# Four moves in VectorE's program order in the attention part of a decoder step

## The chip, the cores and the metric

The kernel runs on one core of a Trainium2 chip. The metric is the device time of one execution in microseconds (us). Engines in the rows: PE is TensorE (matmuls and transposes), PEld its weight loads, DVE VectorE, ACT ScalarE, POOL GpSimd, SP SyncE, whose queue issues the DMAs. Each engine runs its own program in the written order and meets the others at semaphores.

## The reference

One decoder layer for 1024 prompt tokens and for 8 sample tokens, each of which looks back at 1024 cached positions in 8 pages of 128. What matters here is the attention of the prompt, and the scores of the cached pages:

```python
z = h @ w_in                                   # q, k, v of 4 differential and 8 forgetting heads
q1, q2, ka = rope(q1), rope(q2), rope(k)       # rotation, differential heads alone
a  = softmax(q1 k1^T) - lam * softmax(q2 k2^T);  oa = a @ v        # differential group
s  = q k^T + C[t] - C[s];                        of = softmax(s) @ v   # forgetting group
# each sample token: the same against its 8 cached pages, C from the cached log gates
x  = x + rmsnorm(concat(rmsnorm(oa), of) @ w_o)
x  = x + rmsnorm((gelu(conv(h @ w_gate)) * (h @ w_up)) @ w_down)
```

Everything is float32; the large products are made as three products of a high and a low part.

## The kernel before, in words

All four engines walk through the same 64 jobs, `for J in range(NJ + 3)`. Job J is the block of 128 queries `tile(J) = J % 8` against the keys up to it, in unit `unit(J) = J // 8`. A unit is a pair of head maps. Units 0 to 3 are the differential heads, units 4 to 7 the forgetting heads (`fox(J)`, J from 32 on). A job's work is spread over several rounds:

- TensorE in round J: the scores of job J (line 1361), half chunks of the input projection of a later unit (line 1271), transposes of keys and values into rows (1385), the weighted sum of job J-2 (1413, or 1410 in the forgetting units), small matmuls for the sample tokens (1423 to 1443), value pages (1455), and at the round's end the transposes of job J-1's weights (`turn`, 1397). In the forgetting units the result of job J-3 is turned back (1495), and the second map of job J-2 is transposed near the round's start.
- VectorE in round J: the row maxima of job J (1120), the reciprocals and scales of job J-1 (`weights`, 1087 to 1096), the scaled result rows of job J-2 (`rows_out`, 1109 or 1106), in the forgetting units the copies of the second map's transposed weights (`turned`, 1127, into `a_t`), and the reduction of one key page (1044).
- ScalarE: exponentials (859), copies of the first map's transposed weights (853), the copies of the projection's chunks out of PSUM (745 to 755), their half swap (764) and rows (836, 847).
- GpSimd: the product of each key page with the queries (`multiply`, 641, four pieces to a page), the sums of log gates over later pages (`later_pages`, 652), low parts of weights (614), and from unit 1 on the rotations.

Two things tie the order of these together. First, nearly all small results of TensorE go through two PSUM banks in turn, in the order of a list `ring`. TensorE takes the bank of entry n only when entry n-2 has been copied out (`bank(e)`, `wait_evacuated`). In a round the end of the list is: the weighted sum `("o", J-2)`, the small sample entries, the page sums `("fb", b)`, then one or two entries for the transposes of job J-1, one for each four blocks. So the second of two such entries lies in the bank of `("fb", b)`, if there is one in that round. Page sums fall in rounds 4, 11, 18, 25, 32, 39, 46 and 54. Second, key pages lie in two buffers: a page is loaded when the page before the last has been reduced, multiplied by GpSimd, then reduced by VectorE in a fixed round.

The keys of unit 1 are projected in rounds 0 to 2, and VectorE rotates them (`rope`, lines 974 to 978, three instructions to a third). `behind_first` names rounds 39, 47 and 55, whose page work is done in the round that follows, behind the first maximum.

Of the kernel before, what the change touches and what calls it, by code (L numbers as in the profile page):

```python
# [29 lines left out]
PAGES = 8  # L30
PAST = PAGES * P
NPOOL = DB * PAGES * 5 // 4
MAPS = 8
# [129 lines left out]
def project(nc, io, place):  # L163
# [117 lines left out]
    NJ = MAPS * NT  # L281
# [96 lines left out]
    def bank_of(e):  # L378
        return PS[:, 4 + X[e] % 2, :]
# [57 lines left out]
    with nc.Block() as block:  # L437
# [503 lines left out]
        def _(dve):  # L941
# [181 lines left out]
            def turned(J):  # L1123
                for e in turns_of(J, 1):
                    _, _, m, c, nblk = e
                    dve.wait_ge(x_done, X[e] + 1)
                    dve.tensor_copy(at[:, m, c:c + nblk, :], bank_of(e)[:, 0:nblk * P].rearrange("p (k q) -> p k q", q=P)).then_inc(dve_evac, 1)
# [21 lines left out]
            def pages_and_norms(J):  # L1149
                for g in range(2, EARLY_PAGES) if J == 0 else k_pages(J - 1):  # L1150
                    if not late_page(g):
                        reduce_page(g)
                for b in at_job(J, 1):
                    page_maxima(b)

            behind_first = [4 * NT + NT - 1, 5 * NT + NT - 1, 6 * NT + NT - 1]
            for J in range(NJ + 3):
                if J >= 3 and fox(J - 3):
                    rows_out(J - 3)
                if J < LAST_UNIT:  # L1160
                    maximum(J, 0)
                if J - 1 in behind_first and J < LAST_UNIT:
                    pages_and_norms(J - 1)
                if 2 <= J < NJ + 2 and fox(J - 2):
                    turned(J - 2)
                if LAST_UNIT <= J < NJ:
                    maximum(J, 0)
                if J - 1 in behind_first and J == LAST_UNIT:
                    pages_and_norms(J - 1)
                if J < NJ:  # L1170
                    maximum(J, 1)
                if 1 <= J <= NJ:
                    weights(J - 1)
                if 2 <= J < NJ + 2 and not fox(J - 2):
# [21 lines left out]
                if J == 1:  # L1196
# [1 line left out]
                    dve.wait_ge(w_hi_done, n + 1)  # L1198
                    dve.wait_ge(w_lo_done, n)
                    dve.tensor_tensor(w_lo[:, n % 2], w_raw[:, n % 2], w_hi[:, n % 2].bitcast(F32), ALU.subtract).then_inc(w_lo_done, 1)  # L1200
                if 1 <= J <= 3:
                    rope(chunk_of(k_tile(1), J - 1))
                if J < NJ:
                    for e in soft_at(J):
                        if e[0] == "fb":
                            dve.wait_ge(x_done, X[e] + 1)
                            if e[1]:
                                dve.wait_ge(fb_added, e[1])
                            dve.tensor_copy(gate_sum.rearrange("p n m -> p (n m)"), bank_of(e)[:, 0:PAGES * MAPS]).then_inc(dve_evac, 1)
                        elif e[0] == "mt":  # L1210
                            row_maximum(e[1])
                        elif e[0] == "nm":
# [1692 lines left out]
```

## Time and profile before

| | before |
|---|---|
| median of 3 runs | 1432.31 us (1429.55 to 1434.42) |
| the profiled execution, its own time | 1437.39 us |
| its span, first to last instruction | 1434.4 us |
| mean granted clock of TensorE | 0.996 of full |
| granted clock of TensorE from 480 to 500 us | 1.00 of full |
| TensorE matmuls, busy | 1393.1 us, 97% |
| VectorE, busy | 896.3 us, 62% |

The span is one execution; the runs are timed without the profiler. 3.0 us of the profiled execution lie outside its span. The attention rounds go from about 148 us to about 620 us of the span. An instruction's row gives its start, its duration, and in brackets how long its engine had been idle before it and what ended that. Starts on one engine may lie up to some tenths of a microsecond ahead of the end of the instruction before, since the ends are partly drain.

### The profile page before, as it was taken

The page shows a single profiled execution, that of the slowest core. Times are in us where ns is not written, and L with a number is a line of the kernel's source. Part 1 is how long each engine was busy: PE and PEld are TensorE (multiplying, and loading weights), DVE is VectorE, ACT ScalarE, POOL GpSimd, SP SyncE. Part 2 cuts the span into 40 slices and gives each one's busy share as a digit, 9 for nine tenths or more (in the row PEclk, how much of TensorE's full clock was granted, in tenths as well). Part 3 has the DMA queues.
Part 4 walks back from the last instruction along what each step waited for, and adds up shares of the span by engine and source line. Part 5 has one row for each costly group of instructions (what it writes and reads, how often), then busy time and mean ns, then how long its engine had stood idle before and what let it go on. Part 6 is the DMA issues. An engine that isn't in the chain of part 4 may idle for free. (4 is left out here: it accounts for less than half of the span.)

```text
span 1434.4 us, 27861 instructions
## 1 busy us (share of the span) xinstructions
PE 1393.1 (97%) x10628; PEld 1256.8 (88%) x10628; DVE 896.3 (62%) x1437; ACT 630.6 (44%) x1216; POOL 521.0 (36%) x727
## 2 busy tenths in 40 slices
PE   7999999999999999899999999999999998999998
PEld 6999877877777777577899899999999998999998
DVE  6421767667565654675459767766776657654685
ACT  7743655554454454633334423332333223444552
POOL 4223777765555650011103143344332425100052
PEclk9999999999999999999999999999999999999999
DMA  6113557777767663531322254555454527656773
GB/s 193 45 50 90 177 165 223 220 233 253 249 199 223 200 218 93 199 133 61 103 83 89 82 155 141 154 155 157 137 151 141 155 97 251 176 164 197 231 257 109
DMA packets 219390, 229.78 MB, mean 160 GB/s; under 512 B 24739, under 2 KB 151531, under 8 KB 219220
## 3 DMA queue, kind: packets, MB, share of 16 engines
q1 hardware_dynamic: 219258, 228.01, 51.5%
q8 instruction: 84, 1.38, 0.4%
q14 instruction: 48, 0.39, 0.1%
HBM read 181.06 MB, written 46.99 MB: 159 GB/s over the span
## 5 line engine op out<-in xcount | busy, mean ns | idle before, releaser
L641 POOL TENSOR_TENSOR k_page<-k_page,q_bc 128x256 f32<-128x256 f32 x256 | 184.9, 754 | 136.7 <-DMA k_page<-in_cache_fox_k 101.3
L1271 PE MATMUL PS<-ht_hi,w_hi 128*128 128x344 f32 x576 | 193.9, 337 | 2.3 <-DVE ht_lo L950 1.4
L1271 PE MATMUL PS<-ht_hi,w_lo 128*128 128x344 f32 x576 | 184.6, 320 | 0.0
L1271 PE MATMUL PS<-ht_lo,w_hi 128*128 128x344 f32 x576 | 184.3, 320 | 0.0
L2772 PE MATMUL PS<-act_hi,wd_hi 128*128 128x258 f32 x616 | 140.8, 287 | 7.7 <-DVE act_lo L2575 7.1
L859 ACT ACTIVATE probs<-probs,stat 128x256 f32<-128x256 f32 (+7 forms) x128 | 98.5, 771 | 98.7 <-DVE stat L1120 98.0
L2772 PE MATMUL PS<-act_hi,wd_lo 128*128 128x258 f32 x616 | 139.0, 284 | 0.0
L2772 PE MATMUL PS<-act_lo,wd_hi 128*128 128x258 f32 x616 | 138.8, 284 | 0.0
L1271 PEld LDWEIGHTS PS<-ht_hi,w_hi 128*128 128x128 f32 x576 | 109.0, 189 | 27.3 <-issue 20.3
L2720 PE MATMUL PS<-ht_hi,wgu_hi 128*128 128x258 f32 x608 | 122.7, 283 | 0.0
L2720 PE MATMUL PS<-ht_lo,wgu_hi 128*128 128x258 f32 x608 | 122.5, 283 | 0.0
L2720 PE MATMUL PS<-ht_hi,wgu_lo 128*128 128x258 f32 x608 | 122.5, 283 | 0.0
L2349 ACT ACTIVATE conv<-gate,conv_consts 128x1032 f32<-128x1032 f32 x22 | 27.5, 1252 | 206.3 <-DVE gate L2537 186.3
L2772 PEld LDWEIGHTS PS<-act_hi,wd_hi 128*128 128x128 f32 x616 | 102.1, 191 | 9.2 <-DVE act_lo L2575 9.2
L1271 PEld LDWEIGHTS PS<-ht_lo,w_hi 128*128 128x128 f32 x576 | 108.9, 189 | 0.0
L1271 PEld LDWEIGHTS PS<-ht_hi,w_lo 128*128 128x128 f32 x576 | 108.6, 189 | 0.0
L2772 PEld LDWEIGHTS PS<-act_lo,wd_hi 128*128 128x128 f32 x616 | 102.2, 190 | 0.0
L2772 PEld LDWEIGHTS PS<-act_hi,wd_lo 128*128 128x128 f32 x616 | 102.0, 191 | 0.0
L1044 DVE TENSOR_REDUCE scores<-k_page 128x16 f32<-128x1024 f32 x64 | 77.3, 1210 | 33.0 <-POOL k_page L641 33.0
L2720 PE MATMUL PS<-t_hi,wgu_hi 128*128 128x258 f32 x456 | 93.1, 286 | 3.5 <-DVE u L2537 3.5
L2720 PEld LDWEIGHTS PS<-ht_hi,wgu_lo 128*128 128x128 f32 x608 | 94.3, 189 | 0.0
L2720 PEld LDWEIGHTS PS<-ht_hi,wgu_hi 128*128 128x128 f32 x608 | 94.3, 190 | 0.0
(311 smaller groups left out, 3357.8 us busy)
## 6 DMA issues: line engine op xcount, KB each, us to landing
b_dram<-conv SPq DMA_DIRECT2D x77, 258.0 KB, 3.1
k_page<-in_cache_diff_k SPq DMA_DIRECT2D x64, 256.0 KB, 2.9
k_page<-in_cache_fox_k SPq DMA_DIRECT2D x64, 256.0 KB, 3.4
v_page<-in_cache_diff_v SPq DMA_DIRECT2D x64, 256.0 KB, 2.8
v_page<-in_cache_fox_v SPq DMA_DIRECT2D x64, 256.0 KB, 3.0
act_raw<-b_dram SPq DMA_DIRECT2D x55, 258.0 KB, 2.7
w_raw<-in_w_in SPq DMA_DIRECT2D x24, 512.0 KB, 5.3
wgu_raw<-in_w_gate SPq DMA_DIRECT2D x22, 512.0 KB, 4.5
```

Source lines behind the costliest of these rows:

```text
L641: ins = pool.tensor_tensor(kpage[:, g % 2, c:c + PIECE], kpage[:, g % 2, c:c + PIECE], qbc[:, c:c + PIECE], ALU.mult)
L859: act.activation(p, p, ACT.Exp, bias=stat[:, J % 8, m:m + 1], scale=-1.0, accum_out=stat[:, J % 8, 2 + m:3 + m]).then_inc(exp_done, 1)
L1044: dve.tensor_reduce(scores[:, b % 3, :, n, :], kpage[:, g % 2, :].rearrange("p (k m c) -> p k m c", k=2, c=HD), AX, ALU.add).then_inc(red_ ...
L1271: ins = pe.matmul(PS[:, z_bank(c), 0:THIRD], b[:, k, :], a[:, k, third(i)], start=(k == 0 and p == 0), stop=(k == KC - 1 and p == 2))
L2349: act.activation(cbuf[:, f % 2, :], gb[:, f % 2, 2:2 + TOK], ACT.Identity, bias=bias[:, f:f + 1], scale=taps[2][:, f:f + 1]).then_inc(c_in ...
L2720: ins = pe.matmul(PS[:, bank + piece, 0:PART], w[:, k, :], a[:, k, piece * PART:(piece + 1) * PART], start=first and k == 0 and m == 0, st ...
L2772: ins = pe.matmul(PS[:, bank_of(r, d) + piece, 0:PART], w[:, d * P:(d + 1) * P], a[:, first + piece * PART:first + (piece + 1) * PART], st ...
```

## The change

Only VectorE's program is written in another order; no instruction is added or taken away.

1. The three rotations of unit 1's keys move from the ends of rounds 1, 2 and 3 to rounds 2, 3 and 4, behind both maxima and ahead of the reciprocals.
2. In all rounds with page sums but 39, the copy of the page sums (`gate_sums`) moves behind the page reductions of that round.
3. In rounds 40 and 48 the copies into `a_t` (`turned(J - 2)`) move ahead of the page reduction and of what follows it.

```diff
@@ def pages_and_norms(J)
                 for b in at_job(J, 1):
+                    if J not in behind_first:
+                        gate_sums(("fb", b))
                     page_maxima(b)
+
+            def gate_sums(e):
+                dve.wait_ge(x_done, X[e] + 1)
+                if e[1]:
+                    dve.wait_ge(fb_added, e[1])
+                dve.tensor_copy(gate_sum..., bank_of(e)[:, 0:PAGES * MAPS]).then_inc(dve_evac, 1)
@@ for J in range(NJ + 3)
                 if J < LAST_UNIT:
                     maximum(J, 0)
+                if 2 <= J < NJ + 2 and fox(J - 2):
+                    turned(J - 2)
                 if J - 1 in behind_first and J < LAST_UNIT:
                     pages_and_norms(J - 1)
-                if 2 <= J < NJ + 2 and fox(J - 2):
-                    turned(J - 2)
...
                 if J < NJ:
                     maximum(J, 1)
+                if 2 <= J <= 4:
+                    rope(chunk_of(k_tile(1), J - 2))
                 if 1 <= J <= NJ:
                     weights(J - 1)
...
-                if 1 <= J <= 3:
-                    rope(chunk_of(k_tile(1), J - 1))
                 if J < NJ:
                     for e in soft_at(J):
                         if e[0] == "fb":
-                            dve.wait_ge(x_done, X[e] + 1)
-                            ...
+                            if J in behind_first:
+                                gate_sums(e)
```

VectorE, end of round 3 and start of round 4, before: the rotation (974 to 978), the page reduction (1044), the maxima of job 4 (1120), then the weights of job 3.

```order
L1109 TENSOR_SCALAR q_t_64<-PS,stat_106 128x128
L974 TENSOR_TENSOR z_raw_104<-z_raw_104,cos_81 128x344
L975 TENSOR_TENSOR z_swapped_105<-z_swapped_105,sin_82 128x344
L978 TENSOR_TENSOR k_t_70<-z_raw_104,z_swapped_105 128x344
L1044 TENSOR_REDUCE scores_99<-k_page_95 128x2x8
L1120 ISA probs_77,stat_106<-PS,zeros_mask_86 128x640
L1120 ISA stat_106 128x1
L1120 ISA probs_77,stat_106<-PS,zeros_mask_86 128x640
L1120 ISA stat_106 128x1
L1087 RECIPROCAL stat_106<-stat_106 128x2
```

The same place in the changed kernel:

```order
L1109 TENSOR_SCALAR q_t_64<-PS,stat_106 128x128
L1044 TENSOR_REDUCE scores_99<-k_page_95 128x2x8
L1120 ISA probs_77,stat_106<-PS,zeros_mask_86 128x640
L1120 ISA stat_106 128x1
L1120 ISA probs_77,stat_106<-PS,zeros_mask_86 128x640
L1120 ISA stat_106 128x1
L974 TENSOR_TENSOR z_raw_104<-z_raw_104,cos_81 128x344
L975 TENSOR_TENSOR z_swapped_105<-z_swapped_105,sin_82 128x344
L978 TENSOR_TENSOR k_t_70<-z_raw_104,z_swapped_105 128x344
L1087 RECIPROCAL stat_106<-stat_106 128x2
```

The rotation stands now between the maxima and the weights; rounds 2 and 3 read the same with other widths.

VectorE, end of round 32, before: the scaled rows (1109), the copy of the page sums, the reduction of the last page of sample token 4, its maxima, and job 33.

```order
L1109 TENSOR_SCALAR q_t_64<-PS,stat_106 128x128
L1209 COPY sample_gate_sums_59<-PS 128x64
L1044 TENSOR_REDUCE scores_99<-k_page_95 128x2x8
L1050 TENSOR_TENSOR scores_99<-scores_99,sample_gate_sums_59 128x64
L1054 TENSOR_REDUCE page_max_122<-scores_99 128x16
L1120 ISA probs_77,stat_106<-PS,gate_34_83 128x256
```

The same place in the changed kernel:

```order
L1109 TENSOR_SCALAR q_t_64<-PS,stat_106 128x128
L1044 TENSOR_REDUCE scores_99<-k_page_95 128x2x8
L1162 COPY sample_gate_sums_59<-PS 128x64
L1050 TENSOR_TENSOR scores_99<-scores_99,sample_gate_sums_59 128x64
L1054 TENSOR_REDUCE page_max_122<-scores_99 128x16
L1120 ISA probs_77,stat_106<-PS,gate_34_83 128x256
```

The copy, which gives TensorE its bank back, stands behind the reduction. In rounds 4, 11, 18, 25 and 54 it is the same; in round 46 two reductions stand ahead of it.

VectorE, start of round 48, before: the first maximum, the reduction, the two copies into `a_t`, the second maximum.

```order
L1120 ISA probs_77,stat_106<-PS,gate_34_83 128x128
L1120 ISA stat_106 128x1
L1044 TENSOR_REDUCE scores_99<-k_page_95 128x2x8
L1127 COPY a_t_80<-PS 128x512
L1127 COPY a_t_80<-PS 128x384
L1120 ISA probs_77,stat_106<-PS,gate_35_84 128x128
```

The same place in the changed kernel:

```order
L1120 ISA probs_77,stat_106<-PS,gate_34_83 128x128
L1120 ISA stat_106 128x1
L1127 COPY a_t_80<-PS 128x512
L1127 COPY a_t_80<-PS 128x384
L1044 TENSOR_REDUCE scores_99<-k_page_95 128x2x8
L1120 ISA probs_77,stat_106<-PS,gate_35_84 128x128
```

The copies stand ahead of the reduction. In round 40 the page sums' addition and maxima stand there too, and they move with the reduction.

## Rows read from the trace of the kernel before

**Rows 1.** The page's first part: busy time, share of the span, instructions.

```profile
PE 1393.1 (97%) x10628; PEld 1256.8 (88%) x10628; DVE 896.3 (62%) x1437; ACT 630.6 (44%) x1216; POOL 521.0 (36%) x727
```

**Rows 2.** TensorE's waits, 145 to 600 us: releaser, total, times, longest.

```profile
PE PS L1397 <- DVE q_t L1109: 1.7, 2, 1.1
```

**Rows 3.** Timeline of VectorE, rounds 1 to 4: start, duration, instruction, idle time.

```profile
158.77 1.03 DVE L974 TENSOR_TENSOR z_raw<-z_raw,cos 128x344 f32<-128x344 f32 x1
161.66 1.21 DVE L1044 TENSOR_REDUCE scores<-k_page 128x16 f32<-128x1024 f32 x1
...
163.74 0.15 DVE L1087 RECIPROCAL stat<-stat 128x2 f32<-128x2 f32 x1
164.24 0.48 DVE L1096 SCALAR_TENSOR_TENSOR probs<-probs,stat 128x256 f32<-128x256 f32 x1
164.90 0.51 DVE L974 TENSOR_TENSOR z_raw<-z_raw,cos 128x344 f32<-128x344 f32 x1
...
171.59 1.21 DVE L1044 TENSOR_REDUCE scores<-k_page 128x16 f32<-128x1024 f32 x1
173.16 0.83 DVE L1120 CUSTOM_DVE_ANT_0 probs<-PS,zeros_mask 128x640 f32<-128x640 f32 x1 [0.35 <-PE PS L1361]
174.65 0.16 DVE L1087 RECIPROCAL stat<-stat 128x2 f32<-128x2 f32 x1
176.25 0.35 DVE L1109 TENSOR_SCALAR q_t<-PS,stat 128x128 f32<-128x128 f32 x1 [0.35 <-PE PS L1413]
```

**Rows 4.** Timeline of GpSimd: a page multiplied in round 1, the next token's first.

```profile
156.27 4.13 POOL L641 TENSOR_TENSOR k_page<-k_page,q_bc 128x256 f32<-128x256 f32 x4 [1.99 <-DMA k_page<-in_cache_fox_k]
...
179.78 0.74 POOL L641 TENSOR_TENSOR k_page<-k_page,q_bc 128x256 f32<-128x256 f32 x1 [5.44 <-DMA q_bc<-qs_dram]
```

**Rows 5.** Timeline of TensorE: transposes at the ends of rounds 2, 4, 5.

```profile
165.09 0.41 PE L1397 MATMUL PS<-ident,probs 128*128 128x128 f32 x2 [1.27 <-ACT sample_rows L836]
177.30 0.66 PE L1397 MATMUL PS<-ident,probs 128*128 128x128 f32 x4
183.68 0.74 PE L1397 MATMUL PS<-ident,probs 128*128 128x128 f32 x5 [1.15 <-DVE q_t L1109]
```

**Rows 6.** VectorE's waits, 140 to 600 us, columns as in rows 2.

```profile
DVE sample_gate_sums L1209 <- PE PS L1425: 17.8, 8, 3.0
```

**Rows 7.** Timeline of GpSimd, TensorE and VectorE, end of round 32.

```profile
372.59 2.77 POOL L641 TENSOR_TENSOR k_page<-k_page,q_bc 128x256 f32<-128x256 f32 x4
373.84 1.09 PE L1397 MATMUL PS<-ident,probs 128*128 128x128 f32 x8
373.94 0.22 DVE L1209 COPY sample_gate_sums<-PS 128x64 f32<-128x64 f32 x1 [1.98 <-PE PS L1425]
375.39 1.22 DVE L1044 TENSOR_REDUCE scores<-k_page 128x16 f32<-128x1024 f32 x1 [1.23 <-POOL k_page L641]
```

**Rows 8.** The same engines, end of round 46.

```profile
479.57 2.78 POOL L641 TENSOR_TENSOR k_page<-k_page,q_bc 128x256 f32<-128x256 f32 x4
481.53 0.88 PE L1397 MATMUL PS<-ident,probs 128*128 128x128 f32 x6
```

**Rows 9.** Timeline of VectorE and TensorE, start of round 48.

```profile
494.50 1.22 DVE L1044 TENSOR_REDUCE scores<-k_page 128x16 f32<-128x1024 f32 x1 [2.06 <-POOL k_page L641]
494.48 0.31 PE L1271 MATMUL PS<-ht_hi,w_lo 128*128 128x344 f32 x1
496.38 0.33 PE L1385 MATMUL PS<-ident,v_t 128*128 128x128 f32 x1 [1.58 <-DVE a_t L1127]
```

**Rows 10.** Timeline of TensorE, round 40.

```profile
430.42 0.31 PE L1271 MATMUL PS<-ht_hi,w_lo 128*128 128x344 f32 x1
430.87 0.66 PE L1385 MATMUL PS<-ident,v_t 128*128 128x128 f32 x4
```

**Rows 11.** Timeline of TensorE, the longest wait ahead of 830 us.

```profile
824.15 0.80 PE L2720 MATMUL PS<-t_hi,wgu_hi 128*128 128x258 f32 x2 [3.52 <-DVE u L2537]
```

**Rows 12.** A stretch: length; busy (instructions) by engine; granted clock, DMA share, GB/s.

```profile
824.20:834.00 9.80, 9.80 (x61) 9.80 (x62) 7.94 (x8) 1.98 (x3) 6.05 (x3) 0.72 0.48 146
```

More of the change, by code:

```diff
@@ L1153, in pages_and_norms @@
                 for b in at_job(J, 1):
+                    if J not in behind_first:
+                        gate_sums(("fb", b))
                     page_maxima(b)
+            def gate_sums(e):
+                dve.wait_ge(x_done, X[e] + 1)
+                if e[1]:
+                    dve.wait_ge(fb_added, e[1])
+                dve.tensor_copy(gate_sum.rearrange("p n m -> p (n m)"), bank_of(e)[:, 0:PAGES * MAPS]).then_inc(dve_evac, 1)
             behind_first = [4 * NT + NT - 1, 5 * NT + NT - 1, 6 * NT + NT - 1]
@@ L1205, in _ @@
                         if e[0] == "fb":
-                            dve.wait_ge(x_done, X[e] + 1)
-                            if e[1]:
-                                dve.wait_ge(fb_added, e[1])
-                            dve.tensor_copy(gate_sum.rearrange("p n m -> p (n m)"), bank_of(e)[:, 0:PAGES * MAPS]).then_inc(dve_evac, 1)
+                            if J in behind_first:
+                                gate_sums(e)
                         elif e[0] == "mt":
```

## The prediction

> **What bounds the kernel now.** I read the page's first part before anything else: TensorE is busy for 97% of the span [rows 1]. A change on VectorE can then give or take only what TensorE waits for VectorE, so the second view was TensorE's own waits over the attention rounds. They are short and few: two waits for scaled rows, 1.7 us together, and one wait for the a_t copies, 1.58 us [rows 2, 9]. I then laid the timelines of TensorE, VectorE and GpSimd beside each other at every place at which the program order differs, and asked two questions: what stands now behind what, and which of these does TensorE need next. Waits of VectorE itself cost nothing where TensorE does not follow. I worked with start times on TensorE: starts of back-to-back matmuls of a chunk lie about 0.15 us apart, and a start that comes later than that is a delay even where no idle time is printed.
>
> **The rotations, rounds 2 to 4.** No instruction is added. VectorE does the same work per round, so the weights of a round would come at the same time, were it not for two places.
>
> Round 1 ends before with the rotation from 158.77 and the reduction at 161.66, which waited for nothing [rows 3]. Now the reduction comes first. Its page is being multiplied from 156.27 for 4.13 us, to 160.40 [rows 4]; with VectorE still for the last piece I take 160.2. From the reduction's start to the reciprocal it was 163.74 - 161.66 = 2.08 us with the two maxima between, so the rotation starts at 162.3. A rotation's first instruction took 1.03 us beside the multiplication and 0.51 us at 164.90 [rows 3]; three of a kind make 2.9 us (158.77 to 161.66) or 1.5. Half of it lies beside the next page's multiplication: 2.0 us, to 164.3, so the weights come 0.5 us later. The weights were ready at 164.24 + 0.48 = 164.72, the transposes at 165.09 waited for ScalarE's sample rows [rows 3, 5], which come earlier now with the maxima. TensorE then starts at about 165.4: 0.3 us later (bounds 0 and 1.2, by a rotation of 2.9 us).
>
> Round 4 is the dearer one. Before, the maxima of job 4 waited for TensorE's scores until 173.16, 0.35 us after the reduction, with all three rotations done [rows 3]. The scores do not come sooner, so what now stands in front of them leaves VectorE idle, and the third rotation, 1.5 us, falls wholly behind them. The reciprocal at 174.65 goes to 174.65 + 0.3 + 1.5 = 176.45. The scaled rows started at 176.25 after a wait of 0.35 us for TensorE, without it 1.25 us behind the reciprocal; now nothing is left to wait for, and they start at 177.7 and end at 178.05. The transposes at the end of the round need the bank that these rows leave (entry n-2), and TensorE starts about 0.14 us after such an end (183.68 in round 5 is such a start). So 178.1 or 178.2 (instructions overlap a little) for a start that was 177.30 [rows 5]: **+0.8 us**, the 0.3 us of round 2 included. In the rounds that follow each job's maxima wait for that job's scores, and the 0.8 us stays. Bounds: +0.5 us, if nothing of round 2 is left; +2.2 us, if the third rotation too takes 2.9 us. Who else waits for a rotation: ScalarE's copy of the third chunk needs the first rotation, but stands behind the exponentials of job 2 and the sample rows; unit 1 starts four rounds later. I cost both at nothing; if ScalarE's copy were uncovered, TensorE would wait for it at the next chunk.
>
> This is also where a rule of the Trainium skill bears. The row says: 1.03 us beside GpSimd's multiplication, 0.51 us without [rows 3, 4]. "GPSIMD Engine Reference", in its table of the engine's properties, says that GpSimd shares its SBUF interfaces with VectorE and contends with VectorE's instructions that have two SBUF inputs, as the rotation's have. The trace agrees. By this rule the price hangs on what GpSimd does in the new places; in round 4 it waits for queries, so by the rule 0.8 us stands, and were it multiplying there it would be 2.2 us.
>
> **The page sums.** The reduction now stands ahead of the copy, and the copy gives back the bank that the second entry of the round's last transposes needs. VectorE waited for the page sums 17.8 us in the eight rounds, 2.2 us on the mean [rows 6]. Where the page is ready early, the reduction's 1.2 us fit into that wait, and the copy comes when it came: rounds 11, 18, 25 and 54, whose reductions waited for nothing. I cost them at nothing, since TensorE waits for no maximum there; without that cover each second entry would wait up to 1.2 us. In round 4 there is one entry only; nothing. Two rounds are otherwise.
>
> Round 32: the last page's multiplication runs from 372.59 to 375.36, so the reduction cannot start before 375.39; the copy was done at 373.94 + 0.22 = 374.16 [rows 7]. Now it starts one reduction later, 1.14 us from start to start, at 376.53, is done at 376.75, and TensorE can go on at 376.89. The eight transposes from 373.84 take 1.09 us, so the fifth, which needs the bank, started at about 374.31. **+2.6 us.** The cover is gone, since the multiplication is itself late. Queued behind the copy on VectorE: page maxima and the maxima of job 33, whose scores TensorE makes later by as much.
>
> Round 46: multiplication to 479.57 + 2.78 = 482.35, the first of two reductions fits ahead; the second starts at 482.38, the copy at 483.52, done 483.74, TensorE at 483.88. Of the six transposes from 481.53 the fifth started at about 482.02 [rows 8]. **+1.9 us.**
>
> Bounds for both together: 0, if the pages are multiplied in time, and 4.5 us. GpSimd's pace is set by loads that follow VectorE's reductions and SP's rounds, which follow TensorE, so I expect it to shift with TensorE and take 4.5.
>
> The rule that speaks loudest against this part: "Perfetto Trace Analysis", in its part on the TensorE timeline, says that VectorE is strict FIFO. The trace shows it: the reduction waits 1.23 us in round 32 and the addition behind it starts only after it [rows 7]. By the rule the copy waits for GpSimd and the sum is as above; if the engine let the copy pass, the 4.5 us would be nothing.
>
> **The a_t copies.** Round 48: the reduction waited 2.06 us for its page, to 494.50, with the copies behind, and TensorE's next transposes, whose bank the first copy leaves, started at 496.38 instead of 494.48 + 0.15 = 494.63 [rows 9]. Their input, the round's first transposes, is long made by then. **-1.75 us.** What is late next is the chunk itself, so all of it is won. Round 40: 430.87 instead of 430.57 [rows 10]: **-0.3 us**. Bounds: -2.05 and 0.
>
> **Sum.** 0.8 + 2.6 + 1.9 - 1.75 - 0.3 = +3.2 us. On the profiled execution 1437.39 + 3.2 = 1440.6; its time is 5.1 us above the median of the runs, so for the median 1432.31 + 3.2 = 1435.5.
>
> **Rivals.**
> - *TensorE's clock falls at the new gap.* Behind a wait of 3.52 us the granted clock was 0.72 over the next 9.8 us, which is half speed (1.2 instead of 2.4 GHz) for 2 x 0.28 x 9.8 = 5.5 us, a loss of 2.7 us [rows 11, 12]. Behind the 1.58 us in round 48 it stayed at 1.00 (table of the times). The new gap of 2.6 us lies between. Then 1435.5 + 2.7 = 1438.2.
> - *A rotation beside a multiplication.* GpSimd gets its queries earlier and the third rotation takes 2.9 us instead of 1.5: 1435.5 + 1.4 = 1436.9. Against it: it waited for them until 179.78 [rows 4], three microseconds behind the place.
> - *The pages come in time.* Earlier reductions in rounds 11 to 25 free buffers earlier. Had the multiplications of rounds 32 and 46 ended 1.2 us before the page sums, the 4.5 us would not be paid: 1432.31 + 0.8 - 2.05 = 1431.1. Against it: the pace is set anew in each round.
> - *Faster: the earlier maxima break the chain of rounds 4 to 7.* If the maxima of the early rounds, freed of the rotations, let ScalarE and the scaled rows come early enough, the 0.8 us is not paid and the waits of rounds 5 and 6, 1.7 us [rows 2], go; with the pages in time it is 1432.31 - 1.7 - 2.05 = 1428.6. It decides at the point at which round 4's scores stop being what the maxima wait for. Against it: the row says that they are.
> - *No effect at all*, if TensorE's delays are taken up further on: its later waits are for VectorE and ScalarE work that itself follows TensorE, so I give this little; 1432.3.
>
> **How the numbers follow.** Chances: my forecast 0.46, clock 0.19, slow rotation 0.08, pages in time 0.14, faster 0.07, no effect 0.06. A change below 0.3% (4.3 us) cannot be told from none here; the three runs before alone span 4.9 us. With about 2 us of scatter between two medians, slower by over 4.3 us comes out in 0.3 of the forecast, 0.75 of the clock's case, 0.55 of the slow rotation's: 0.14 + 0.14 + 0.04, and with a little for costs I do not see, 0.37. Faster by over 4.3 us: 0.4 of the faster case and little of the pages': 0.07. The rest, 0.56, is no difference to be told. The range takes in all but the tails: 1430.5 to 1440. The forecast's own range is 1433 to 1438.
>
> **What would show it.** In the changed kernel's trace: a wait of TensorE at 1397 of about 2.5 us in round 32 and 1.8 us in round 46, each put down to the copy of the page sums; in round 4 a wait of about 0.5 to 0.8 us for the scaled rows; the wait for the a_t copies gone from the list; the reductions of rounds 11, 18, 25 and 54 ahead of the copies in VectorE's idle time. I am wrong if round 32 or 46 shows no such wait, or if the waits of rounds 5 to 7 grow or vanish.

## The result, and the profile after

| | before | changed |
|---|---|---|
| median of 5 runs each, us | 1432.31 | 1443.09 |
| lowest to highest, us | 1429.55 to 1434.42 | 1440.62 to 1446.59 |
| ratio, with its 95% interval | | 1.0065 (1.005 to 1.0081) |
| the profiled execution, us | 1437.39 | 1446.59 |
| its span, us | 1434.4 | 1444.3 |
| its mean granted clock | 0.996 | 0.993 |

The changed kernel is 0.65% slower. I had said 1435.5 us, with 1440 as the upper end, so the time lies outside my range. In three later comparisons the kernel before had medians of 1433.48 (29 runs), 1433.63 (29) and 1433.61 (24); in the last of them the changed kernel, run again, took 1441.2 us (7 runs), a ratio of 1.0046 (1.0029 to 1.0062).

First part of the page of the changed kernel, to lay beside [rows 1]:

```profile
PE 1398.5 (97%) x10628; PEld 1261.0 (87%) x10628; DVE 892.2 (62%) x1437; ACT 630.9 (44%) x1216; POOL 518.6 (36%) x727
```

The counts are the same, and yet TensorE is busy for 5.4 us longer (1398.5 against 1393.1). Waits alone can't do that. The same matmuls ran more slowly somewhere. The three falls of the clock shown below make up 5.1 us of it.

TensorE's waits from 145 to 600 us, and below them VectorE's for the page sums (releaser, total, times, longest):

```profile
PE PS L1403 <- DVE sample_gate_sums L1162: 4.7, 2, 2.3
PE PS L1403 <- DVE q_t L1109: 2.0, 3, 1.1
...
DVE sample_gate_sums L1162 <- PE PS L1431: 7.5, 5, 1.9
```

Line 1403 is line 1397 of before. It has a new releaser at the head of the list, the copy of the page sums, two times 2.3 us. The wait for the scaled rows went from 1.7 us in two to 2.0 in three [rows 2]. VectorE's own wait for the page sums went from 17.8 us in eight to 7.5 in five [rows 6]. In rounds 32 and 46 VectorE now idles ahead of the reduction instead (3.04 and 3.19 us, in the fences below), and the copy that TensorE needs stands behind that.

GpSimd, TensorE and VectorE at the end of round 32, to lay beside [rows 7]:

```profile
374.11 2.77 POOL L641 TENSOR_TENSOR k_page<-k_page,q_bc 128x256 f32<-128x256 f32 x4
375.33 0.66 PE L1403 MATMUL PS<-ident,probs 128*128 128x128 f32 x4
376.91 1.22 DVE L1044 TENSOR_REDUCE scores<-k_page 128x16 f32<-128x1024 f32 x1 [3.04 <-POOL k_page L641]
378.05 0.21 DVE L1162 COPY sample_gate_sums<-PS 128x64 f32<-128x64 f32 x1
378.32 0.86 PE L1403 MATMUL PS<-ident,probs 128*128 128x128 f32 x4 [2.33 <-DVE sample_gate_sums L1162]
```

Before, the eight transposes were one block. Now four start at 375.33 and the fifth at 378.32. The fourfold block takes 0.66 us, so the fifth would have started at about 375.8: a delay of 2.5 us from start to start, where I had 2.6. The chain stands in the fence: multiplication to 376.88, reduction to 378.13, copy to 378.26, TensorE at 378.32. The page sums themselves were done by 375.40, when their last matmul ended (374.97 and 0.43 us). The copy did not pass the waiting reduction, as my forecast had assumed.

The same at the end of round 46, to lay beside [rows 8]:

```profile
485.79 2.77 POOL L641 TENSOR_TENSOR k_page<-k_page,q_bc 128x256 f32<-128x256 f32 x4
487.00 0.66 PE L1403 MATMUL PS<-ident,probs 128*128 128x128 f32 x4
488.58 1.22 DVE L1044 TENSOR_REDUCE scores<-k_page 128x16 f32<-128x1024 f32 x1 [3.19 <-POOL k_page L641]
489.72 0.21 DVE L1162 COPY sample_gate_sums<-PS 128x64 f32<-128x64 f32 x1
489.99 0.44 PE L1403 MATMUL PS<-ident,probs 128*128 128x128 f32 x2 [2.33 <-DVE sample_gate_sums L1162]
```

Also 2.5 us, where I had 1.9. The multiplication starts 1.21 us ahead of the transposes (485.79 and 487.00). Before it was 1.96 us (479.57 and 481.53). TensorE's transposes come 5.47 us later than before, and the multiplication 6.22 us: GpSimd fell back by 0.75 us more than TensorE.

What follows on these waits stands in the stretches of the changed kernel (length; busy and instructions of PE, PEld, DVE, ACT, POOL; granted clock; DMA share; GB/s):

```profile
374.00:378.00 4.00, 1.58 (x10) 1.23 (x10) 1.09 (x1) 0.97 (x2) 2.88 (x5) 1.00 0.13 49
378.00:382.00 4.00, 3.68 (x17) 2.80 (x18) 1.73 (x9) 2.38 (x5) 1.53 (x3) 0.58 0.91 322
488.00:492.00 4.00, 2.01 (x8) 1.04 (x10) 1.96 (x4) 0.68 (x2) 0.55 (x1) 0.91 0.76 226
492.00:496.00 4.00, 4.00 (x23) 2.91 (x20) 2.07 (x5) 0.60 (x1) 0.00 (x0) 0.66 0.78 236
600.00:604.00 4.00, 1.68 (x17) 0.89 (x15) 3.22 (x7) 1.30 (x5) 0.00 (x0) 0.99 0.90 328
604.00:608.00 4.00, 4.00 (x15) 2.28 (x16) 1.31 (x3) 3.19 (x6) 0.00 (x0) 0.58 0.55 223
```

TensorE works 1.58 us of 4, and right behind it the granted clock is 0.58: half speed for most of the stretch, 0.42 x 4 = 1.7 us lost. Behind round 46 it is 0.09 x 4 + 0.34 x 4 = 1.7 us. Before, both places read 1.00. A third fall, here also 1.7 us, stands at 604 us, in round 62, behind this wait for a value page of the samples (a timeline of SyncE, which issues the load, and of TensorE):

```profile
594.72 0.62 SPq L510 DMA_DIRECT2D v_page<-in_cache_fox_v  x1
601.82 0.61 PE L1461 MATMUL PS<-v_page,scores 128*4 128x256 f32 x8 [1.76 <-DMA v_page<-in_cache_fox_v]
```

Before, the same load was issued at 587.29, and the matmuls started at 592.57 without a wait.

Round 4 of the changed kernel, VectorE and TensorE, to lay beside [rows 3, 5]:

```profile
174.09 0.82 DVE L1120 CUSTOM_DVE_ANT_0 probs<-PS,zeros_mask 128x640 f32<-128x640 f32 x1 [1.20 <-PE PS L1367]
175.58 0.52 DVE L974 TENSOR_TENSOR z_raw<-z_raw,cos 128x344 f32<-128x344 f32 x1
176.99 0.16 DVE L1087 RECIPROCAL stat<-stat 128x2 f32<-128x2 f32 x1
178.16 0.34 DVE L1109 TENSOR_SCALAR q_t<-PS,stat 128x128 f32<-128x128 f32 x1
178.65 0.52 PE L1403 MATMUL PS<-ident,probs 128*128 128x128 f32 x3 [0.35 <-DVE q_t L1109]
```

The rotation stands behind the maxima at the short duration, 0.52 us, and the transposes wait for the scaled rows. This is the step as I described it. In round 2 the same order made TensorE's transposes wait 1.22 us for the weights (166.00), where before they had waited 1.27 us for ScalarE (165.09) [rows 5]. Taking off the 0.7 us that job 1 was already late, that is 0.2 us, where I had said 0.3.

Start of round 48, to lay beside [rows 9]:

```profile
501.82 1.16 DVE L1127 COPY a_t<-PS 128x512 f32<-128x512 f32 x2 [0.17 <-PE PS L1403]
502.89 1.21 DVE L1044 TENSOR_REDUCE scores<-k_page 128x16 f32<-128x1024 f32 x1
503.68 0.32 PE L1277 MATMUL PS<-ht_hi,w_lo 128*128 128x344 f32 x1
503.83 0.60 PE L1391 MATMUL PS<-ident,v_t 128*128 128x128 f32 x4
```

The transposes of the values follow 0.15 us behind the last matmul of the chunk; before it was 1.90 us. Mark that the reduction behind the copies waits for nothing either. Its page had been ready, which it was not before. That becomes the second finding below.

To follow the difference along the program I took the start of each job's first maximum on VectorE, changed less before. The differences of +0.95 and +0.70 us in jobs 0 and 1 were there before any moved instruction had run. They are scatter between two executions. The -0.71 us of job 2 is the edit: the rotation no longer stands ahead of that maximum.

| job | 4 | 31 | 34 | 36 | 46 | 47 | 49 | 62 | 63 |
|---|---|---|---|---|---|---|---|---|---|
| us | +0.9 | +1.4 | +5.6 | +5.2 | +5.2 | +9.2 | +7.4 | +7.4 | +10.0 |

Rounds 32 and 46 cost 4.2 us (job 31 to 34) and 4.0 us (46 to 47) in this execution, and each is a wait of 2.5 and a clock loss of 1.7, within 0.2 us. Round 48 gives back 1.8. Round 62 costs 2.6 in this execution. The span is 9.9 us longer.

### The profile page after: what moved, and what is told of

It reads as the page before. It is cut to its first block and busy times, and to the rows that moved or that the text cites. A ratio compares the mean times of both kernels' runs of the same rounds, so it can differ in the third digit from the quotient of the medians.

```text
span 1444.3 us, 27861 instructions
## 1 busy us (share of the span) xinstructions
PE 1398.5 (97%) x10628; PEld 1261.0 (87%) x10628; DVE 892.2 (62%) x1437; ACT 630.9 (44%) x1216; POOL 518.6 (36%) x727
## 5 line engine op out<-in xcount | busy, mean ns | idle before, releaser
L2726 PEld LDWEIGHTS PS<-ht_lo,wgu_hi 128*128 128x128 f32 x608 | 94.2, 189 | 0.0
```

Of the source, the lines that this page charges most:

```text
L2726: ins = pe.matmul(PS[:, bank + piece, 0:PART], w[:, k, :], a[:, k, piece * PART:(piece + 1) * PART], start=first and k == 0 and m == 0, st ...
```

## The experiments

The one theory, A: the time is the two waits for the bank, plus a fall of TensorE's clock behind each. The rival, B: the waits are as seen, and the rest is something else of the order (earlier reductions, other load times, the feed-forward stage). Its variant, C: the rotations or the copies carry more than I gave them. All ratios are to the kernel before, run beside. "Lost to the clock" is (1 - mean granted clock) x span, as a mean over the runs. It also counts time in which TensorE idles at half clock, which costs nothing: before, 0.7 us of the fall behind 820 us lie in the wait itself (granted clock 0.84 from 820 to 824.2). It was 3.75, 4.1 and 4.0 us for the kernel before in the three comparisons, and 8.65 for the changed kernel in the first one.

| kernel | ratio (95% interval) | mean against before, us | lost to the clock, us |
|---|---|---|---|
| e1_rotations_alone | 1.0012 (0.9997 to 1.0027) | +1.6 | 4.5 |
| e2_sums_alone | 1.0048 (1.0034 to 1.0063) | +6.3 | 9.35 |
| e3_copies_alone | 0.9998 (0.9987 to 1.0008) | -0.3 | 3.5 |
| e4_after_filled | 1.0024 (1.0012 to 1.0036) | +3.8 | 4.4 |
| e5_sums_ahead_in_32_46 | 0.9992 (0.9978 to 1.0007) | -0.3 | 3.8 |
| e6_before_filled | 1.0018 (1.0006 to 1.0031) | +2.1 | 4.8 |
| e7_copies_ffn_filled | 1.0005 (0.9994 to 1.0017) | +0.8 | 3.8 |
| e8_sums_32_alone | 1.0037 (1.0025 to 1.0050) | +5.5 | 6.0 |
| e9_changed_again | 1.0046 (1.0029 to 1.0062) | +6.9 | 8.4 |
| e10_rotations_and_sums | 1.0038 (1.0024 to 1.0052) | +5.3 | 7.4 |
| e11_before_filled_copies | 1.0008 (0.9994 to 1.0021) | +1.6 | 3.9 |
| e12_changed_filled_7 | 1.0021 (1.0010 to 1.0032) | +3.1 | 4.8 |

### The three parts, one at a time

e1 keeps the move of the rotations and nothing else:

```diff
+                if 2 <= J <= 4:
+                    rope(chunk_of(k_tile(1), J - 2))
-                if 1 <= J <= 3:
-                    rope(chunk_of(k_tile(1), J - 1))
```

> The kernel before with the three rotations moved and nothing else. Theory (three parts that add up, the page sums being the dear one): +0.6 us, as rounds 2 to 7 of the changed kernel's trace show (first maximum of job 7 there 1.28 us later than before, of which 0.70 us lie ahead of round 1); the median within 0.3% of before. Rival (the rotations set off something in later rounds): +3 us or more. In the trace a wait of TensorE for the scaled rows of about 0.5 to 0.8 us at the end of round 4.

From job 1 to job 5 the first maxima fell back by 0.54 us (-0.59 to -0.05). The median is 1.4 us up, but its interval (-0.4 to +3.9 us) still includes zero. In the changed kernel run again the same two jobs give +0.63. The rotations are worth 0.5 to 0.6 us.

e2 moves the copy of the page sums alone:

```diff
                 for b in at_job(J, 1):
+                    if J not in behind_first:
+                        gate_sums(("fb", b))
                     page_maxima(b)
```

> The kernel before with the copies of the page sums behind the reductions, but for round 39, and nothing else. Theory: TensorE waits 2.3 us in round 32 and 2.3 us in round 46 for its bank, and behind each wait the granted clock falls to half for 3.4 us, 1.7 us each: +8 us, with or without the clock +4.5 to +8. Rival (the waits are taken up further on, or the rest of the loss is of another part): under +4 us.

TensorE's waits in e2, 145 to 600 us:

```profile
PE PS L1403 <- DVE sample_gate_sums L1162: 4.7, 2, 2.3
...
PE PS L1391 <- DVE a_t L1127: 0.3, 1, 0.3
```

The same two waits, the same clock loss (9.35 us against 3.75), and most of the whole change's cost (+6.3 us, inside the 4.5 to 8 that I expected). C falls. The second line is the surprise. The a_t copies were not moved, and yet the wait of 1.58 us for them [rows 9] is not in the list. The 0.3 us that is left is round 40's, at 432.82. Start of round 48 in e2, VectorE and TensorE:

```profile
497.56 1.22 DVE L1044 TENSOR_REDUCE scores<-k_page 128x16 f32<-128x1024 f32 x1
498.69 1.15 DVE L1127 COPY a_t<-PS 128x512 f32<-128x512 f32 x2
499.66 0.32 PE L1277 MATMUL PS<-ht_hi,w_lo 128*128 128x344 f32 x1
499.82 0.60 PE L1391 MATMUL PS<-ident,v_t 128*128 128x128 f32 x4
```

The reduction waits for nothing, since all was delayed by round 46 and its page was done by then (GpSimd's multiplication ended at 492.49 + 2.81 = 495.30). TensorE goes on 0.16 us behind the last matmul of the chunk, without a wait. So the old order costs TensorE nothing there. The difference to before went from 5.19 us at job 48 to 3.38 at job 49, -1.81 with no copy moved.

e3 moves the a_t copies alone:

```diff
+                if 2 <= J < NJ + 2 and fox(J - 2):
+                    turned(J - 2)
                 if J - 1 in behind_first and J < LAST_UNIT:
                     pages_and_norms(J - 1)
-                if 2 <= J < NJ + 2 and fox(J - 2):
-                    turned(J - 2)
```

> The kernel before with the a_t copies ahead of the page reduction in rounds 40 and 48, and nothing else. Theory: the wait of 1.58 us for the a_t copies is gone, first maximum of job 49 about 1.8 us earlier than before by the round: -1.9 us at the median, nothing lost elsewhere. Rival (the won time is waited away in the next rounds): 0, with new waits of TensorE between rounds 49 and 63.

In its trace job 48 to 49 goes from -0.52 to -2.32 us, -1.80, and nothing takes it back up to the end of the attention rounds; the span is 1429.6. The medians of 12 and 29 runs show 0.2 us of that. The interval (-1.9 to +1.1 us) holds both. So the step is seen in the trace and its worth at the end isn't established. One reason may be that the wait of 1.58 us is read from one execution of the kernel before; nothing on record shows how long it is in the others.

### Keeping the clock

e4 is the changed kernel with TensorE kept at work in the two waits. It writes 14 matmuls into a bank that nobody reads then, ahead of the fifth transpose:

```diff
+                    if (J, m, c) in ((31, 0, 4), (45, 0, 4)):
+                        pe.wait_ge(max_done, 2 * s_free[J + 2])
+                        for _ in range(14):
+                            pe.matmul(PS[:, s_bank[J + 2], 0:THIRD], ht_hi[:, 0, 0:P], ht_hi[:, 0, 0:THIRD], ...)
                     dst = bank(e)
```

> The changed kernel in which TensorE, at the two places where it waits for its bank (rounds 32 and 46), first issues 14 matmuls of 128x344 that write to a PSUM bank which the next scores overwrite; nothing reads them. 14 x 0.157 us = 2.2 us, so they fit into the wait of 2.3 us. Theory (the idle time lets the clock fall): the waits' delay stays, the granted clock in both places stays at 1.00, and the kernel is about 3.4 us faster than the changed one: +7 us against before in place of +10.8. Rival (the clock falls for another reason, or the loss behind the waits is not the clock's): as slow as the changed kernel, +10.8, or slower by the added matmuls.

The filling in round 32 of e4 (timeline of TensorE), and the stretches there and at round 46:

```profile
374.98 0.66 PE L1407 MATMUL PS<-ident,probs 128*128 128x128 f32 x4
375.39 2.46 PE L1404 MATMUL PS<-ht_hi 128*128 128x344 f32 x14
377.99 0.44 PE L1407 MATMUL PS<-ident,probs 128*128 128x128 f32 x2
```

```profile
378.00:382.00 4.00, 4.00 (x31) 3.58 (x32) 1.47 (x7) 2.58 (x7) 1.53 (x3) 1.00 0.84 277
488.00:492.00 4.00, 4.00 (x26) 2.51 (x27) 1.89 (x4) 0.38 (x1) 0.00 (x0) 1.00 0.94 295
```

The fifth transpose still starts 3.0 us behind the first, as in the changed kernel (375.33 to 378.32): the delay is the same, and the clock reads 1.00 where it read 0.58. Counted as above, the two rounds cost +2.3 and +2.9 us instead of 4.2 and 4.0. On the mean 4.4 us are lost to the clock instead of 8.65, and the time is +3.8 us instead of +6.9 (e9) or +10.8 (the first comparison's medians). I had expected +7, which went by the first comparison alone. The gain has the expected size, 3.1 us against e9, and A's second half stands. The clock loss is 4.0 us less than in e9, a little more than two falls of 1.7, and what the rest is was not told apart. Its profiled execution itself is a long one (1442.28 us). Round 62 waited 2.0 us for the value page there and the clock fell behind that, for 3.4 us. More on it below.

e6 puts the same 14 matmuls into the kernel before, where there was no wait (edit as in e4, nothing else).

> The kernel before with the same 2 x 14 filling matmuls at the same places of TensorE's program, where it does not wait. Theory: they cost their own time, 28 x 0.157 = 4.4 us, clock as before. Against this the filled changed kernel is to be read: there the same matmuls made it faster. Rival (the filling changes the time in another way, say through the scores' bank or the order of TensorE's work): clearly more or less than 4.4 us.

The job table shows +2.17 and +2.22 us in the two rounds, and then -1.80 from job 48 to 49: net +2.6, the measured median difference is 1435.52 - 1433.63 = 1.9 (0.9 to 4.4 by the interval). I had expected +4.4 and forgotten the gift of round 48, though e2 had just shown it. It is the cleanest evidence for it, since the delay is made by TensorE alone and no VectorE instruction is moved: the wait of 1.58 us is gone from this trace.

e12 is e4 with 7 matmuls instead of 14.

> The changed kernel with 7 filling matmuls at each of the two places, which leave a wait of about 1.2 us. Theory (the clock falls behind idle time near the 2.3 us of the two waits and does not behind 1.6 us or less): clock and time as with 14 matmuls, +3.5 to +5 us against before. Rival (half the filling saves half the clock's loss): +6 to +7 us, mean clock 0.9955.

TensorE's waits in e12, 370 to 500 us, and two stretches:

```profile
PE PS L1407 <- DVE sample_gate_sums L1162: 2.4, 2, 1.2
```

```profile
374.00:378.00 4.00, 2.75 (x21) 2.06 (x20) 2.42 (x7) 1.59 (x3) 0.57 (x1) 1.00 0.46 147
484.00:488.00 4.00, 2.81 (x17) 1.65 (x17) 1.96 (x4) 0.88 (x2) 0.71 (x2) 1.00 0.81 244
```

Two waits of 1.2 us are left and the clock holds at 1.00, also in the stretches behind them (376 to 380 and 486 to 490 us). Seven matmuls do what fourteen do: ratios of 1.0021 and 1.0024, no difference that the intervals would show. Its +3.1 us on the mean lie a little below the 3.5 to 5 that I expected, and far from the rival's 6 to 7. Round 32 is the test of the idle time. Without filling the clock fell behind it in all five traces that have the wait (changed, e2, e8, e9, e10), and with filling in neither of two. Behind round 46 it held in both with filling, and in two of four without.

### The two rounds, one at a time

e5 is the changed kernel, but the copy stays ahead of the reductions in rounds 32 and 46:

```diff
-                    if J not in behind_first:
+                    if J not in behind_first + [32, 46]:
...
-                            if J in behind_first:
+                            if J in behind_first + [32, 46]:
```

> The changed kernel with the copy of the page sums ahead of the reduction again in rounds 32 and 46 alone; rotations, a_t copies and the page sums of rounds 4, 11, 18, 25 and 54 as changed. Theory (the loss is what TensorE waits in these two rounds and the half clock behind it): both waits and both clock falls are gone, at or below the kernel of the rotations alone: -1 to +1.5 us against before, mean granted clock as before. Rival (reductions ahead of the copy cost in the other rounds too): +4 us or more.

No wait for the page sums is left in TensorE's list. The difference by jobs goes from -0.4 to +0.5 us between jobs 32 and 36, where it went from +1.9 to +5.2 in the changed kernel, and the time is that of before (0.9992, 0.9978 to 1.0007). All of the measurable loss comes with two copies out of eight; the moves in rounds 4, 11, 18, 25 and 54 cost nothing that can be measured, as I had costed them. B falls for everything but what follows from these two rounds.

e8 moves the copy in round 32 alone, in a kernel that is otherwise before's:

```diff
-                    if J not in behind_first:
+                    if J not in [4, 11, 18, 25, 39, 46, 54]:
```

(and the second condition in the same way, with the rotations and a_t copies where they were).

> The kernel before with the copy of the page sums behind the reduction in round 32 alone. Theory: one wait of 2.3 us and in most executions one fall of the clock, 1.7 us: +3 to +4 us, half of what both rounds make. Rival (the two rounds' waits are one, the second following from the first): +6 us, with a wait in round 46 too.

Stretches of e8, the first with the wait, the last two without one:

```profile
374.00:378.00 4.00, 2.47 (x13) 1.58 (x13) 1.96 (x4) 1.32 (x2) 0.29 (x2) 0.69 0.61 205
...
484.00:488.00 4.00, 3.86 (x27) 2.32 (x27) 3.74 (x7) 0.87 (x2) 1.51 (x3) 1.00 0.87 256
488.00:492.00 4.00, 4.00 (x47) 3.23 (x45) 3.19 (x8) 2.36 (x4) 0.00 (x0) 1.00 0.84 261
```

From job 32 to 34 the trace shows +3.6 us, and 1.9 us more than before are lost to the clock on the mean, one fall's worth. In the trace the fall stands where the wait is (0.69) and not in round 46 (1.00), where the old order was kept. The measured +5.5 is over my 3 to 4. The trace has 2.5 us more in round 62, behind a wait of 2.2 for the value page, and that execution is one of the five. The times don't share the loss out evenly between the two rounds. Round 32 alone gives +5.5 us and both together +6.3 (e2), with intervals of about 2 us to either side. That each costs half is read from the job table, not from the times.

### Does anything of the copies remain?

e9 is the changed kernel again, e10 the changed kernel with the a_t copies back behind the reduction (e3's edit undone), e11 is e6 with e3's edit.

> The changed kernel as it is, beside the next three on one chip. Theory (two waits of 2.3 us and their clock falls, 1.7 us each, rotations 0.6 us, less 1.8 us that round 48 gives back): +8 to +10 us against before, mean clock 0.994. Rival (the first comparison was of a slower chip): +6 us or less.

> The changed kernel without the move of the a_t copies in rounds 40 and 48. Theory (the delay of round 46 has by itself given the late page of round 48 its time, as in the run of the page sums alone, where the first maximum of job 49 came 1.8 us less late than that of job 48): the same time as the changed kernel, within 1 us. Rival (the move of the copies is worth 1.8 us beside the rest, as my sum had it): 1.8 us slower than the changed kernel.

> The kernel before with the 2 x 14 filling matmuls and the a_t copies moved. Theory (the filling of round 46 already gives round 48 its 1.8 us, so the copies add nothing): as the filled kernel before, +2.6 us. Rival (both add): +0.8 us.

Round 46 in e9, TensorE's timeline and the stretches around it:

```profile
485.25 0.66 PE L1403 MATMUL PS<-ident,probs 128*128 128x128 f32 x4
488.25 0.44 PE L1403 MATMUL PS<-ident,probs 128*128 128x128 f32 x2 [2.34 <-DVE sample_gate_sums L1162]
```

```profile
484.00:488.00 4.00, 1.90 (x18) 1.23 (x10) 1.16 (x2) 0.60 (x1) 2.81 (x5) 1.00 0.64 152
488.00:492.00 4.00, 3.75 (x24) 2.26 (x25) 1.79 (x6) 0.38 (x1) 0.00 (x0) 1.00 0.84 283
```

The changed kernel came out at +6.9 us on the mean and +7.6 at the median. That is under the 8 to 10 of my theory and over the 6 of the rival (a slower chip in the first comparison). The ratios of the two comparisons, 1.0065 (1.0050 to 1.0081) and 1.0046 (1.0029 to 1.0062), overlap, and no cause for the difference is shown.

It is the same kernel with the same wait of 2.34 us in round 46, and this time the clock did not fall. It did in round 32 of the same execution. Taking all profiled executions with these waits (changed, e2, e8, e9, e10), the clock fell behind round 32 in five of five. Behind round 46 it fell in two of four: in the changed kernel and e2, not in e9 and not in e10, whose wait was 2.03 us. So A has to be put more weakly. A fall behind such a wait comes in some executions and not in others; it is no fixed price.

At the median e10 is 2.1 us (0.15%) below e9 and not above it, outside the 1 us that I had given and on the side away from the rival; the two intervals overlap. Its trace gives -1.80 us from job 48 to 49 (6.76 to 4.96) with the copies where they were. On top of the page sums the moved copies win nothing. e11 says the same from the other side. Job 48 to 49 gives -1.80 in e6 and in e11: it can be given back only once. Its time doesn't decide. +1.6 us on the mean lies halfway between the theory's +2.6 and the rival's +0.8, and e6 had +2.1.

### Inconclusive: the fall that was there before

e7 took e3 and was meant to keep the clock behind the wait of 3.52 us ahead of 824.15 [rows 11, 12], with 22 matmuls in the feed-forward stage:

```diff
+                    for _ in range(22):
+                        pe.matmul(PS[:, Y, 0:PART], w_hi[f % 2][:, A11, 0, :], ht_hi[:, 0, 0:PART], ...)
```

> The kernel before with the a_t copies moved (as in the run of the copies alone) and 22 matmuls of 128x258, read by nothing, ahead of TensorE's wait of 3.52 us in the feed-forward part (line 2720, behind which the clock was at half for 6.8 us). Theory: 22 x 0.12 = 2.6 us of filling fit into the wait, no half clock follows, up to 3.4 us less than the copies alone: -3 to -5 us against before, mean clock 0.998 to 1.0. Rival (the clock falls there for the small rest of the gap, or the wait moves on): as the copies alone, within 1.5 us of before.

Timeline of TensorE in e7, the filling and the wait, and the stretch behind the wait:

```profile
793.03 2.85 PE L2736 MATMUL PS<-ht_hi,wgu_hi 128*128 128x258 f32 x22
...
824.67 0.80 PE L2720 MATMUL PS<-t_hi,wgu_hi 128*128 128x258 f32 x2 [2.79 <-DVE u L2537]
```

```profile
824.00:828.00 4.00, 3.33 (x15) 3.33 (x16) 4.00 (x6) 2.69 (x4) 0.00 (x0) 0.57 0.00 0
```

The edit missed its place. The 22 matmuls ran from 793.03 to 795.88 us, and the wait began at 821.89, 26 us behind their end. They stand ahead of an earlier product that the same line 2720 issues. So the wait was not filled: 2.79 us are left of it, and 3.24 us in e3, which has no filling. Behind it 0.43 x 4 = 1.7 us were lost and nothing more from 828 us on (1.00). That is no success of the filling either, since e3 lost 1.7 us there too. The time didn't move (1.0005, 0.9994 to 1.0017). Whether filling helps at this wait stays untested.

## Why the prediction was wrong

**The step that failed: the clock.** The term of my sum that was wrong is TensorE's clock behind the two new waits. I counted the waits at their length and the clock behind them at nothing. The clock stood among the rivals with a chance of 0.19 "at the new gap", priced once at 2.7 us. In the profiled execution it fell behind both waits, for 1.7 us each, and over five executions behind seven of nine such waits. I had a fall behind 3.52 us and none behind 1.58, a new wait between, nearer to neither, and took the side on which my sum stood. I should have priced two places, each with its own chance: at even odds 1.7 us, by what was seen 7/9 x 2 x 1.7 = 2.6 us. e4 and e12 show that it is the idle time that does it. On the mean over the runs the changed kernel loses 4.4 us more to the clock than before in the later comparison (8.4 against 4.0). In the first it lost 8.65 us, and the clocks of the runs before are not on record there. What is over the 2.6 or at most 3.4 us of the two places must lie elsewhere, and the falls in round 62 are what the traces show of it. The price of 2.7 us for one fall was read from a stretch that starts at 824.20; from 820 to 832 us the loss is 3.4 us, of which 0.7 lie in the wait. The Trainium skill has the case in "TensorE: Matmul & The Clock Gate", under "A second HAM failure mode: psum-queue depth-cycling": a matmul kernel that cycles through its PSUM banks and idles briefly, and often, between groups of matmuls swings between half and full clock. The waits for a bank here agree with it in kind (2.33 us, then a granted clock of 0.58); here a single such wait was enough in seven of nine cases. I had not weighed that section against my own new waits.

**The two waits.** The mechanism was right: the copy behind the reduction, the reduction behind the multiplication, the bank behind the copy, all in the rows above. Round 32: 2.6 us said, 2.5 measured. Round 46: 1.9 said, 2.5 measured, since I let GpSimd shift with TensorE and it ended 0.75 us later against it. Sum 4.5 said, 5.0 measured.

**The rotations.** +0.8 said, +0.5 to +0.6 measured in two traces (e1, e9). Their place and the short duration were right; the wait for the scaled rows is 0.35 us and not 0.5 to 0.8.

**Page sums elsewhere.** At nothing, and so it is (e5).

**The a_t copies.** -1.75 us said for round 48, -1.8 measured, but the step was wrong all the same. The wait of 1.58 us was for a page that came late against TensorE. A delay of TensorE ahead of it takes it away, as far as the page doesn't come later too. In e1, which moves neither copy, TensorE was 1.28 us later at job 48 than before, the page's multiplication started when it did before (491.58 and 491.56), and 1.29 us came back. In e8 TensorE was 2.6 us later and the page 1.6 (493.14); 1.0 us came back and a wait of 0.56 was left. I counted it beside a delay of two rounds earlier, as if the copies had won it. With round 46's delay in place they win nothing (e2, e6, e10). Round 40's -0.3 us is there at the spot (0.16 us from start to start, before 0.45) and gone one job later: jobs 40 and 41 are 5.20 and 5.24 us behind before. The sum is not changed by that, only the credit. The order would have been better without the page sums, and then the -1.8 us show in the trace (e3), though not in the median.

**The sum with what was measured:** 5.0 for the waits, 4.4 for the clock, 0.6 for the rotations, less 1.8 for round 48, is +8.2 us. Measured: +6.9 on the mean in the later comparison, +10.8 at the medians of the first. The sum lies between them. It overshoots e2 (8.8 against 6.3), e10 (7.0 against 5.3) and e12 (4.6 against 3.1) in the same way. Either part of a delay is taken up further on, or part of the clock's loss falls where TensorE idles; no run tells these apart.

**What stays open: round 62.** TensorE's wait there for a value page of the samples was 1.8 us in the changed kernel and 3.4 in e9; 2.0 in e4, 2.2 in e6 and e8, 3.2 in e12; 1.3, 0.7 and 1.1 in e1, e3 and e11; none in the kernel before, e2, e5, e7 and e10. The clock fell behind it in each of the six where it was 1.76 us or longer. Whether it follows the change is open. e2 and e10 carry the costly part and have none, and e6 has 2.2 us without any moved instruction. But all four traces with the whole change in them (changed, e9, e4, e12) have it. Each of these four executions is also 2.1 to 5.0 us longer than the median of its kernel, so they may be the rarer ones; but the traced execution of the kernel before, without this wait, was 5.1 us above its own. One profiled execution for each kernel can't say how often it comes, and why a load that had landed within 5.3 us (587.29 to 592.57) takes 7.1 (594.72 to 601.82) was not settled. It accounts for 2.6 us of the 9.9 by which the two spans differ, and makes the traces of single executions look worse than the medians.

No kernel here beats the one before by what can be measured. The nearest are e3 (0.9998, 0.9987 to 1.0008) and e5 (0.9992, 0.9978 to 1.0007).

## What to carry to other kernels

Price a new wait of the bounding engine twice, by its length and by what its clock does behind it, and once per place. Where the wait can't be avoided, try a few dead matmuls into a free bank (here seven at each of two waits; some 3 to 4 us, with the falls of other places in it). Then look in the trace whether they ran where you meant them to: those of e7 did not. A copy that gives a bank back belongs ahead of an instruction that waits for a third engine, even if that one has mostly been early: look at the rounds where it is late, they were two of eight. Before a wait downstream is put down as a gain of an edit, ask whether another part of the same change delays the waiting engine by as much, because then it goes anyway.

## What I had not expected of the hardware

- Behind TensorE's waits of 2.03 to 2.34 us for the bank the granted clock fell in seven of nine cases. With one kernel and one wait (2.33 and 2.34 us in round 46, changed and e9) it fell once and held once. It held behind 1.58 us (before), 1.3 (e1) and 1.2 twice (e12).
- Over all 14 traces, from 100 us on, TensorE has 67 waits of 1.15 us or more, for whatever cause. The clock fell behind none of the 23 up to 1.58 us, behind 17 of the 25 from 1.76 to 2.94, and behind all 19 from 3.02 up. The new waits stand in the middle group, where both was seen.
- Each fall behind a wait for the bank costs the same 1.7 us: 0.42 x 4 us at 378, 0.09 x 4 + 0.34 x 4 at 488. Behind other waits it was 1.7 (0.42 x 4 at 604, 0.43 x 4 in e7) or twice that, 3.4, as in round 62 of e4, e9 and e12 and before from 820 to 832 us.
- With seven matmuls in the wait and 1.2 us of it left idle, the clock stayed at 1.00 in both rounds of the one trace (e12).
- One 128x344 addition or multiplication of the rotation on VectorE takes 0.52 us where GpSimd waits and 1.03 beside its page multiplication [rows 3, 4]; in round 4 it ran at 0.52 in its new place, as costed. In round 2 of the changed kernel, where GpSimd multiplied until 163.69, the first instruction, from 163.03, took 1.03 us and the second 0.50.
